# Order of the planned work and the differential scale of a two-part transformer block on one Trainium2 core

## What is computed

```python
for l in range(DEPTH_2):                        # 2
    u = rms_norm(x, norm_pre[l]) @ w_in[l]
    (a_q, a_k, a_v, a_z, b_q, b_kv, b_kr, b_z, c_q, c_k, c_v, c_z, g) = jnp.split(u, split_points, axis=-1)
    oa = diff_attention(...)                    # 4 heads of 128
    oa = (rms_norm(oa, da_subln[l]) * (1.0 - lam_init)).reshape(B, S, DA_WIDTH)
    qm  = rms_norm(b_q, mla_q_norm[l]) @ mla_w_qb[l]        # 256 latents
    kvm = rms_norm(b_kv, mla_kv_norm[l]) @ mla_w_kvb[l]     # 128 latents
    ob = mla_attention(...); oc = sliding_window_attention(...)
    gates = jax.nn.sigmoid(g).reshape(B, S, 3, D_MODEL)
    y = (gates[:, :, 0] * ((oa * silu(a_z)) @ w_br_a[l]) + gates[:, :, 1] * ((ob * silu(b_z)) @ w_br_b[l])
         + gates[:, :, 2] * ((oc * silu(c_z)) @ w_br_c[l]))
    x = x + rms_norm(y @ w_out[l], norm_post[l])
    x = x + jax.nn.sigmoid(x @ w_ple_gate[l]) * (p[l] @ w_ple_proj[l])
```

## Time and profile before

| | |
|---|---|
| runs | 1952.02, 1953.65, 1960.69 us |
| median | 1953.65 us |
| profiled execution, own time | 1967.28 us |
| its span | 1965.3 us |
| mean granted clock of PE | 0.986 |
| PE busy | 1886.9 us (96%) |
| POOL busy | 1520.2 us (77%) |
| ACT busy | 938.8 us (48%) |
| DVE busy | 828.6 us (42%) |

### The profile page before, as it was taken

How to read it: one execution, slowest core, us unless ns; L and a number is a source line. 1 busy time by engine, 2 the same in 40 slices (tenths; PEclk the granted TensorE clock), 3 DMA queues, 4 the chain that set the end, 5 groups by cost and what they waited for, 6 DMA issues and landing times.

```text
span 1965.3 us, 27351 instructions
## 1 busy us (share of the span) xinstructions
PE 1886.9 (96%) x9610; PEld 1543.3 (79%) x9610; DVE 828.6 (42%) x1913; ACT 938.8 (48%) x1473; POOL 1520.2 (77%) x1332
## 2 busy tenths in 40 slices
PE   6999999999999999999999999999899999999998
PEld 5777888777888877788787778877788877778876
DVE  7784110446211245411057731126736344556534
ACT  3455444354444346444434644444437644545742
POOL 6758989885897977697976789796677886767784
PEclk9999999999999999999999999999999999999999
DMA  8444656564666554465545456664545555554442
GB/s 267 124 145 142 202 150 235 172 193 117 197 191 210 156 174 158 151 187 184 202 130 157 153 171 189 198 204 126 167 147 147 171 168 172 163 164 143 143 164 97
DMA packets 184269, 330.54 MB, mean 168 GB/s; under 512 B 12188, under 2 KB 44488, under 8 KB 184136
## 3 DMA queue, kind: packets, MB, share of 16 engines
q1 hardware_dynamic: 176224, 323.21, 53.6%
q10 hardware_dynamic: 7912, 5.59, 0.9%
HBM read 325.35 MB, written 3.41 MB: 167 GB/s over the span
## 4 chain that ended last, share of the span: by engine, by line
PE 82%; DVE 8%; POOL 5%; DMA 2%; issue 2%; ACT 1%; ACTq 0%; DVEq 0%
PE acc L1391 24%; PE acc L1392 23%; PE acc L1398 21%; POOL w_lo L1171 5%; PE tps L1338 4%; PE acc L1413 3%; PE ops L1455 2%; PE acc L1394 2%; PE tps L1431 2%; DMA raw<-in_w_down 1%; DVE QT L1550 1%; PE ops L1350 1%; DVE U L1820 1%; PE acc L1362 1%; PE acc L1364 0%
## 5 line engine op out<-in xcount | busy, mean ns | idle before, releaser
L1171 POOL TENSOR_TENSOR w_lo<-raw,w_hi 128x512 fp32r<-128x512 f32 (+2 forms) x1244 | 1479.6, 1226 | 407.2 <-ACT w_hi L1199 406.3
L1199 ACT CAST w_hi<-raw 128x1024 fp32r<-128x1024 f32 (+2 forms) x624 | 615.4, 991 | 777.7 <-PE acc L1398 597.7
L1391 PE MATMUL acc<-w_hi,xT_hi 128*128 128x512 f32 (+1 forms) x1808 | 692.1, 386 | 13.1 <-issue 3.1
L1392 PE MATMUL acc<-w_lo,xT_hi 128*128 128x512 f32 (+1 forms) x1808 | 670.6, 374 | 0.0
L1398 PE MATMUL acc<-w_hi,xT_lo 128*128 128x512 f32 (+2 forms) x1744 | 508.3, 373 | 1.1 <-DVE xT_lo L1650 1.1
L1391 PEld LDWEIGHTS acc<-w_hi,xT_hi 128*128 128x128 f32 x1808 | 344.4, 190 | 87.7 <-issue 22.8
L1392 PEld LDWEIGHTS acc<-w_lo,xT_hi 128*128 128x128 f32 x1808 | 345.0, 191 | 52.8
L1398 PEld LDWEIGHTS acc<-w_hi,xT_lo 128*128 128x128 f32 x1744 | 319.9, 190 | 60.5 <-DVE xT_lo L1650 2.8
L1710 DVE TENSOR_TENSOR H<-G,acc 128x512 f32<-128x512 f32 (+1 forms) x48 | 30.9, 643 | 334.0 <-PE acc L1398 334.0
L1391 PE MATMUL acc<-w_hi,hT_hi 128*128 128x512 f32 x352 | 139.5, 396 | 5.1 <-POOL w_lo L1171 5.1
L1392 PE MATMUL acc<-w_lo,hT_hi 128*128 128x512 f32 x352 | 137.2, 390 | 0.0
(11 more groups left out here) (196 smaller groups left out, 2011.9 us busy)
## 6 DMA issues: line engine op xcount, KB each, us to landing
raw<-in_w_gate_up SPq DMA_DIRECT2D x160, 512.0 KB, 3.9
raw<-in_w_in SPq DMA_DIRECT2D x104, 512.0 KB, 3.7
raw<-in_w_down SPq DMA_DIRECT2D x88, 512.0 KB, 4.0
raw<-in_w_out SPq DMA_DIRECT2D x48, 512.0 KB, 3.7
raw<-in_w_in_a SPq DMA_DIRECT2D x32, 512.0 KB, 3.7
raw<-in_w_in_b SPq DMA_DIRECT2D x20, 512.0 KB, 3.9
raw<-in_w_mem_kv SPq DMA_DIRECT2D x16, 512.0 KB, 4.4
raw<-in_w_gate_up SPq DMA_DIRECT2D x32, 256.0 KB, 2.8
```

The source lines that it names most:

```text
L1171: ins = nc.gpsimd.tensor_tensor(w_lo[:, r, i, 0:ch.width], raw[:, r, i, 0:ch.width], w_hi[:, slot, i, 0:ch.width].bitcast(F32), ALU.subtract)
L1199: nc.scalar.copy(w_hi[:, u.u % SPLIT, 0:u.nk, 0:u.chunk.width], raw[:, u.u % RAW, 0:u.nk, 0:u.chunk.width]).then_inc(S["hi_ready"], 1)
L1391: nc.tensor.matmul(o, hi[:, tok], wh, start=first_k, stop=False)
L1392: ins = nc.tensor.matmul(o, hi[:, tok], wl, start=False, stop=False)
```

## The change

- The third layer's `v_a` is opened right behind the first values chunk, ahead of the halved heads, in the banks of the default.
- Stages and scales of `rms_pre` have the priority t - 1 in place of 0.
- `sub_scale` forms its scale in a PSUM bank, the half of the last step's `values` bank behind the attention output (17 DVE operations). ACT scales the heads (`sub_norm`, four scalings of 128x128 a tile, priority -1), and `sub_gate` is one multiply of 128x512 a tile.
- The latents of a tile are turned when that tile alone of `used` has been read; the 256 columns of `swc` are opened ahead of `w_qb` and `w_kvb`.
- The projection's chunks take any bank and its second tile is held until the last unit of `w_out` is through; `normed` is set to the number of units before the projection.

```diff
@@ norm_tiles
-            first = p.task("DVE", "stage", Stage(fn + "_scale", fed[t], **st), scale, None, [*fed[t], *taken], prio=0)
+            first = p.task("DVE", "stage", Stage(fn + "_scale", fed[t], **st), scale, None, [*fed[t], *taken], prio=t - 1 if fn == "rms_pre" else 0)
...
-                one = p.stage(apply, fn, [gain.load, first, *also[t]], prio=0, half=half, **st)
+                one = p.stage(apply, fn, [gain.load, first, *also[t]], prio=t - 1 if fn == "rms_pre" else 0, half=half, **st)
@@ the first block's heads
             if kind == 1:
                 chunks = turned_heads([(0, 512), (512, 512), (1024, 512)])
+                vq += copy([v_a], banks=[[(3,)], [(3,)]])
             else:
+                vq += copy([v_a])
                 halved = halved_heads()
-            vq += copy([v_a], banks=[[(3,)], [(3,)]] if kind == 1 else beside)
@@ the second block's differential attention
-        sub = p.task("DVE", "stage", Stage("sub_scale", combined), 3200, None, combined)
-        gated = [p.stage(1500, "sub_gate", [sub, gained[t]], t=t, src=da, dst=da) for t in range(T)]
+        sub = p.stage(3400, "sub_scale", combined, banks=[steps[-1].values])
+        scaled = [p.task("ACT", "sub_norm", (t, da, sub), 1200, "sub_normed", [sub], prio=-1) for t in range(T)]
+        gated = [p.stage(1200, "sub_gate", [scaled[t], gained[t]], prio=-1, t=t, src=da, dst=da) for t in range(T)]
+        steps[-1].values.release = sub
@@ the second block's latents
-            p.tile_batches(low, 0, 2, "s", 0, t, [latent[t]], used)
-            p.tile_batches(low, 2, 1, "s", 2, t, [latent[t]], used)
+            p.tile_batches(low, 0, 2, "s", 0, t, [latent[t]], [used[t]])
+            p.tile_batches(low, 2, 1, "s", 2, t, [latent[t]], [used[t]])
         gone = [*a_turned, steps[-1].values]
+        swc = copy(sw, 512, [(C_CQ + 512, 256)])
...
-        swc = copy(sw, 0, [(C_CQ, 512)])
+        swc = copy(sw, 0, [(C_CQ, 512)]) + swc
...
-        swc += copy(sw, 512, [(C_CQ + 512, 256)])
@@ the second block's end of a layer
-        proj = lin(w["w_ple_proj_2"][l], 2, "s", [(c, n, "copy", (ple_out, c)) for c, n in column_chunks(0, D)])
+        ahead = len(p.units)
+        proj = lin(w["w_ple_proj_2"][l], 2, "s", [(c, n, "copy", (ple_out, c)) for c, n in column_chunks(0, D)],
+                   hold=[[], [out[-1].units[-1].mm[1]]], banks=ANY)
         norm_tiles("rms_post", g, [[ch.take[t] for ch in out] for t in range(T)], "x", out, apply=1500)
+        p.normed = ahead
@@ the scale of the differential attention, on ACT and DVE
+            def sub_norm(t, src, sub):
+                act.wait_ge(S["stage"], sub.n)
+                for i in range(DA_H):
+                    head, c = rows(src)[:, t, P * i:P * i + P], T * i + t
+                    ins = nc.scalar.activation(head, head, ACT.Copy, scale=small[:, 5, c:c + 1])
+                ins.then_inc(S["sub_normed"], 1)
...
+            def rms_columns_in_bank(y, mean, var, eps, ms, bank, done):
+                n = mean.shape[1]
+                a1, r = (bank[:, n * i:n * i + n] for i in range(2))
+                link(v.tensor_copy(a1, mean))
+                link(v.scalar_tensor_tensor(out=a1, in0=a1, scalar=1.0, in1=mean, op0=ALU.mult, op1=ALU.mult))
+                link(v.scalar_tensor_tensor(out=a1, in0=a1, scalar=eps, in1=var, op0=ALU.add, op1=ALU.add))
+                link(v.tensor_copy(ms, a1))
+                link(v.tensor_scalar(r.bitcast(I32), a1.bitcast(I32), -0.5, float(0x5F3759DF), ALU.mult, ALU.add))
+                for i in range(3):
+                    link(v.tensor_copy(y, r))
+                    link(v.scalar_tensor_tensor(out=a1, in0=r, scalar=-0.5, in1=y, op0=ALU.mult, op1=ALU.mult))
+                    link(v.scalar_tensor_tensor(out=a1, in0=a1, scalar=1.0, in1=ms, op0=ALU.mult, op1=ALU.mult))
+                    ins = v.scalar_tensor_tensor(out=r if i < 2 else y, in0=a1, scalar=1.5, in1=y, op0=ALU.add, op1=ALU.mult)
+                    if i < 2:
+                        link(ins)
+                ins.then_inc(done, 1)
...
-                    rms_columns(small[:, 5, 0:8], small[:, 7, :], RMS_EPS, small[:, 5, 8:16], small[:, 3, 8:16])
+                    rms_columns_in_bank(small[:, 5, 0:8], small[:, 7, 0::2], small[:, 7, 1::2], RMS_EPS,
+                                        small[:, 5, 8:16], ops[:, st.banks[0].slot[0], T * P:], done)
                 elif fn == "sub_gate":
-                    for i in range(DA_H):
...
+                    heads = rows(st.dst)[:, t, 0:DA_H * P]
+                    v.tensor_tensor(heads, heads, rows(st.src)[:, t, 1536:2048], ALU.mult).then_inc(done, 1)
```

More of the change, by code:

```diff
@@ L1016, in build @@
             "scores_ready", "logits_ready", "max_ready", "probs_ready", "combined", "pv_ready",
-            "out_hi", "act_normal", "pool_normal",
+            "out_hi", "sub_normed", "act_normal", "pool_normal",
             "out_taken", "out_gated", "maps_mixed", "dve_chain", "index_ready", "index_relu", "index_added", "x_kept")}
@@ L1291, in _ @@
                     output_hi(k.it)
+                elif k.kind == "sub_norm":
+                    sub_norm(*k.it)
                 elif k.kind == "first_constants":
@@ L1814, in do_stage @@
                 elif fn == "sub_scale":
-                    rms_columns(small[:, 5, 0:8], small[:, 7, :], RMS_EPS, small[:, 5, 8:16], small[:, 3, 8:16])
+                    rms_columns_in_bank(small[:, 5, 0:8], small[:, 7, 0::2], small[:, 7, 1::2], RMS_EPS,
+                                        small[:, 5, 8:16], ops[:, st.banks[0].slot[0], T * P:], done)
                 elif fn == "sub_gate":
-                    for i in range(DA_H):
-                        c = T * i + t
-                        head = rows(st.dst)[:, t, P * i:P * i + P]
-                        ins = v.scalar_tensor_tensor(out=head, in0=head, scalar=small[:, 5, c:c + 1],
-                                                     in1=rows(st.src)[:, t, 1536 + P * i:1536 + P * i + P],
-                                                     op0=ALU.mult, op1=ALU.mult)
-                    ins.then_inc(done, 1)
+                    heads = rows(st.dst)[:, t, 0:DA_H * P]
+                    v.tensor_tensor(heads, heads, rows(st.src)[:, t, 1536:2048], ALU.mult).then_inc(done, 1)
                 elif fn == "gain_z":
```

## The result

The changed kernel has a median of 1927.74 us (1925.48 to 1931.1, 4 runs), the kernel before, beside it, 1954.83. The ratio of the runs is 0.9866 (95% interval 0.9847 to 0.9885), 26 us less; the two medians lie 27 apart. A second comparison gave 0.9877 (0.9863 to 0.9892), 24 us less. The forecast was 32 less, 1921.6, with a range of 1909 to 1945. The profiled execution of the changed kernel took 1926.78.

The account below looks back on a forecast made before the run. PE was taken to bound the kernel, busy 1886.9 of 1965.3 us. Terms A to E sum to 35.9 us; less 4, some 32 came off the median 1953.65, giving 1921.6 us, range 1909 to 1945.

Parts of the forecast that it names:

- the allowance of 4 us: Whole kernel: 4 us taken off the summed gain, as the replanned queues can open new waits.
- D: Second block's latents, two places: each tile's latents alone, 256-column chunk moved as cover; gain 4.3 us.
- A: Third layer, norm of the second token tile: `v_a` moved up fills PE's hole; gain 5.3 us.
- B: Projection in both second-block layers: more first-tile units and any bank fill holes of 3.8; gain 11.4 us.
- C: Start of the second block's second layer: changed priority brings the turn 2.1 us ahead; gain 3.7 us.
- E: Differential scale, two places: scale in a bank, heads scaled by ACT; gains 7.3 and 3.9, together 11.2 us.
- Rival 4: Differential scale: operations in the bank wait for POOL, making the kernel 19.5 us slower, 1973.2; chance 0.04.
- Signs: What would show it: PE idle 78 to about 55, waits for `U` and `x_rows` gone, clock near 1.00.
- Rival 1: POOL becomes PE's next wait at the holes; 18 of 35.9 us are lost, 1935.8; chance 0.18.
- Rival 3: Edits of order don't take, B and C give nothing: 1936.8, chance 0.07; together with Rival 1 1948.8, 0.08.
- Rival 2: Third layer's attention lies bare for want of 10.9 us of products beside it: 1932.5; chance 0.08.

Follow-up runs that it names:

- The latents alone: Full change with the 256-column chunk put back between the q and k heads, each tile's latents still by themselves: 0.9863 against the kernel before, 1923.66 us.
- the count alone: Kernel before plus only `normed` set to the number of units before the projection, banks as before: 0.995, 9.8 us less.
- the kernel with A alone: Kernel before plus only the third layer's `v_a` opened ahead of the turned heads: 0.9992, 1.6 us less.
- the one with E alone: Kernel before plus only the differential part (scale in a bank, heads scaled by ACT, one multiply a tile): 0.9943, 11.1 us less.

## Why the prediction was right, and where its terms were not

The sign, the mechanism (holes of PE, each with a low clock behind it) and the range held; the time is 6 us above the forecast, 8 by the second comparison. No part gave clearly more than its term and four gave less: of the sum of 35.9, 19.2 came by the parts alone and 24 by the stretches. What brought this near the forecast is the allowance of 4 us and a range made wide for rivals 1 to 3, none of which came; that it was wide enough for the error in D is luck. Term by term, predicted gain against the part alone and against the stretches:

| part | predicted | alone, median | stretches | what was off |
|---|---|---|---|---|
| A | 5.3 | 1.6 | 4.5 | the hole is filled as worked out; the size is 0.8 too large, by the median more |
| B | 11.4 | 8.4 | 8 | `ANY` leaves 1.2 of idle at each place |
| C | 3.7 | 0.8 | 2 | the wait goes, less comes of it |
| D | 4.3 | -2.7 | -1.9 | latents +4.5, moved chunk -6.4 |
| E | 11.2 | 11.1 | 10.7 | the total; not its two places |

- **E.** 17 operations in 3.5 us: 3.5 measured. The chain was put at 8.1, a sum that leaves out the split of 1.05 named in it, and took 7.4 (1378.24 to 1385.63): no split stood in the way, the eight scalings took 2.45 and not 3.2, and the last multiply 1.24 and not 0.9. By place, the first gave 8.7 where 7.3 was forecast, and the second some 2, not surely E's, where it was 3.9; that the total is met to 0.1 is luck in part. Two bounds came from a bad reading: the 3.19 of L1550 in the earlier trace rows is the mean of four that took 9.61, 0.74, 1.18 and 1.21, so it is the length of none of them. The 1 us that the chain might lose by sources in the bank did not show: a copy of 8 columns took 0.17 from the bank and 0.17 from SBUF, where POOL was not at work. Rival 4 needed POOL in the way of operations on the bank; it is not. The rule of the Trainium skill, SBUF — State Buffer, "SBUF: two separate sides", fits with this: it names as those that lock POOL's port pair both operations with two SBUF inputs and those in a two-port mode. The prediction used only the first half. With the second, the slow copies on SBUF (1.10, 1.22) would have a place, though no run here shows in which mode they ran.
- **D** is the step that failed. The latents alone fill both holes and give 4.5, the 4.3 that was booked for latents and chunk together; so the chunk was not needed as cover. The moved chunk was booked as cover, with "0.5 each time" for what its old place would cost; I looked at what stands beside the chunk at its old and new place, but not at what moves on ACT's queue when products of 5.4 us change places. The waits of before had this eviction with no more than 0.4, so the new wait could not be read off there; what could be read is that ACT's exponentials of a step and the load of 1.28 ahead of a sigmoid would hold up PE if they came first.
- **B.** Which bank the second tile takes was booked as a help ("with `ANY` it takes whichever bank is free"); in the traces it is none. With the count alone 9.8 came by the median and 11 by the stretches (6.0 and 5.0, against the row of A), near the 11.4 that were predicted for count and `ANY` together.
- **C.** The hole was priced with the loss of clock of one execution (0.79 over 8 us); behind the same hole the kernel with A alone had 1.00 and the one with E alone 0.79. The idle time went nearly as foreseen (2.6 to 0.4, and 0.5 elsewhere).
- **Signs.** PE's idle time went from 78 to 54, with 55 foretold, but 7.6 of this is the event in the first 70 us; the change itself took some 16 us of idle time and not 23. That the number was met is luck.
- **Rival 1** did not come: the waits for `w_lo` fell from 8.1 to 5.9. **Rival 3**: the edits of order took. The allowance of 4 us for new neighbourhoods had the right idea and too small a size; one neighbourhood, the chunk's, cost 6.4. **Rival 2** did not come either: the products of the third layer's attention took as long as before.
- The 32 us were taken from the median, not from the profiled execution's 1967.28. That was right: 9 of its 13.6 us above the median lay in the first 70 us. From the profiled time the forecast would have been 1935.3.

## What to carry to other kernels

Price a wait of the bounding engine with its clock, but as a range: at the differential scale waits of 2.85 and 6.06 us had a low clock behind them and one of 1.82 had none, while in the fourth layer's norm the same wait of 1.7 had it in some kernels and not in others. An edit that moves work in a planned order has to be followed on every queue, with the function table loads on ACT's counted in. If operations in a chain of small ones take several times their usual length, look whether they coincide with operations of another engine, here POOL, before shortening the chain; and read a mean in a table of groups only after looking at the single values.

## What the runs showed of the hardware

- One DVE operation with SBUF operands lasted until a run of POOL operations, nine and eleven long, was through, 9.61 and 9.63 us in place of 0.75, in two of fourteen profiled executions. In the small operations of the differential scale DVE and POOL took turns, one operation each (1.1 to 1.3 us).
- The same DVE operations on 8 columns took 0.17 us each beside a busy POOL when the working columns lay in a PSUM bank, and up to 1.3 when they lay in SBUF, copies and a scalar operation with one source among them.
- The loss of clock behind the same hole is not fixed. In the fourth layer's norm PE waits 1.7 us in every kernel; the windows behind it, in the kernel with A alone and in the changed one:

```profile
988.10:996.10 8.00, 5.43 (x27) 4.37 (x27) 7.47 (x23) 0.59 (x1) 1.73 (x2) 0.84 0.23 67
996.10:1004.10 8.00, 8.00 (x30) 6.46 (x29) 3.80 (x17) 3.70 (x5) 4.89 (x4) 0.73 0.50 140
```

```profile
988.40:996.40 8.00, 5.42 (x33) 4.42 (x32) 7.47 (x23) 0.81 (x2) 1.68 (x2) 1.00 0.23 67
996.40:1004.40 8.00, 8.00 (x43) 6.71 (x42) 6.44 (x29) 5.09 (x6) 7.10 (x6) 1.00 0.69 201
```

The idle time is the same, 2.6 in the first window; in one kernel the clock is 0.73 behind it, in the other 1.00. The stretch takes 45.1, 46.6 or 47.8 us, and the two kernels that were profiled twice had the same value both times. Why one kernel gets the one and another the other stays open.
